# Turns of blocks: products with the identity matrix become TensorE transposes

## What is computed

```python
h = rmsnorm(x) * (1 + sc1) + sh1                      # modulation from c @ w_ada
qkv, z, b, a, cq, ckv, kpe, gate_a, gate_b = split(h @ w_in)
y_a = gdn_branch(qkv, z, b, a, ...)                   # short conv, delta rule, gated norm, @ w_o_gdn
y_b = mla_branch(cq, ckv, kpe, ...)                   # latent attention, causal or over pages, @ w_o_mla
x = x + g1 * ((sigmoid(gate_a) * y_a + sigmoid(gate_b) * y_b) @ w_out)
h = rmsnorm(x) * (1 + sc2) + sh2
# experts: top 4 of 32, for each chosen expert e of a token
gu = h @ w_gu[e] + b_gu[e]
gt = minimum(gu[:, :1024], 7); up = clip(gu[:, 1024:], -7, 7)
y = ((up + 1) * gt * sigmoid(1.702 * gt)) @ w_dn[e] + b_dn[e]
x = x + g2 * sum(gate * y)
```

## Time and profile before

| | |
|---|---|
| median of 3 runs | 1608.9 us (1607.83 to 1614.73) |
| span of the profiled execution | 1606.7 us |
| TensorE busy | 1543.6 us, 96% |
| VectorE busy | 481.4 us, 30% |
| ScalarE busy | 343.8 us, 21% |
| moved by the transfers | 541.33 MB, mean 337 GB/s |

### The profile page before, as it was taken

One profiled execution on the slowest core, in us unless ns is written; L12 is line 12 of the kernel. 1 busy time (PEld: TensorE's weight loads), 2 busy tenths in 40 slices (PEclk: granted clock), 3 DMA queues, 4 the chain that ended last, 5 costly groups with the idle time before them and its releaser, 6 DMA issues.

```text
span 1606.7 us, 25500 instructions
## 1 busy us (share of the span) xinstructions
PE 1543.6 (96%) x10185; PEld 845.6 (53%) x10185; DVE 481.4 (30%) x1079; ACT 343.8 (21%) x795; POOL 6.8 (0%) x13
## 2 busy tenths in 40 slices
PE   6999899999999999999999999999999999999997
PEld 4888786776677687434343343343343333333333
DVE  1665456322301025312221222122222212212224
ACT  2333452223311102111111111111111111111113
POOL 0000000000000000000000000000000000000000
PEclk9999999999999999999999999999999999999999
DMA  9748442545499964699999999999999999999991
GB/s 396 323 157 356 182 159 90 226 135 156 138 316 351 350 285 187 262 381 428 429 428 428 430 427 428 429 428 429 427 428 430 427 428 429 424 420 425 425 419 62
DMA packets 60259, 541.33 MB, mean 337 GB/s; under 512 B 7298, under 2 KB 11906, under 8 KB 29346
## 3 DMA queue, kind: packets, MB, share of 16 engines
q1 hardware_dynamic: 59474, 534.65, 81.0%
q0 software_dynamic: 720, 5.76, 0.9%
HBM read 533.54 MB, written 6.84 MB: 336 GB/s over the span
## 4 chain that ended last, share of the span: by engine, by line
PE 72%; DMA 21%; DVE 2%; SPq 2%; issue 2%; ACT 1%; ACTq 0%; DVEq 0%
DMA regC<-biases 20%; PE banks L606 14%; PE banks L558 10%; PE banks L1323 9%; PE banks L873 5%; PE banks L508 4%; PE banks L520 2%; PE banks L594 2%; PE banks L576 2%; PE banks L1156 2%; PE banks L1088 2%; PE banks L972 2%; PE banks L533 1%; DMA ring<-wpre 1%; PE banks L1181 1%
## 5 line engine op out<-in xcount | busy, mean ns | idle before, releaser
L558 PE MATMUL banks<-ring,regA 128*64 128x512 f32 x2024 | 446.8, 594 | 0.7 <-ACT regA L631 0.7
L558 PEld LDWEIGHTS banks<-ring,regA 128*64 128x64 f32 x2024 | 142.2, 137 | 281.9 <-issue 280.9
L606 PE MATMUL banks<-ring,regC 128*64 128x512 f32 x1024 | 226.8, 596 | 0.0
L668 DVE TENSOR_TENSOR regB<-regB,banks 128x528 f32<-128x528 f32 x128 | 81.5, 700 | 351.9 <-PE banks L533 351.9
L606 PEld LDWEIGHTS banks<-ring,regC 128*64 128x64 f32 x1024 | 70.7, 137 | 131.8 <-issue 127.9
L634 ACT ACTIVATE regA<-regA 128x512 f32<-128x512 f32 x32 | 20.1, 630 | 527.5 <-DVE regA L689 527.5
L689 DVE TENSOR_SCALAR regA<-banks 128x512 f32<-128x512 f32 x32 | 22.1, 692 | 347.0 <-PE banks L576 347.0
L508 PE MATMUL banks<-regC,regA 128*64 128x512 f32 (+1 forms) x396 | 97.1, 607 | 0.0
L873 PE MATMUL banks<-hT,ring 128*128 128x264 f32 x384 | 86.5, 387 | 0.0
L873 PEld LDWEIGHTS banks<-hT,ring 128*128 128x128 f32 x384 | 72.7, 190 | 12.7 <-issue 0.4
L533 PE MATMUL banks<-regA,regC 64*128 64x264 f32 x512 | 71.7, 409 | 0.0
(11 more groups left out here) (476 smaller groups left out, 1625.6 us busy)
## 6 DMA issues: line engine op xcount, KB each, us to landing
ring<-w_gu SPq DMA_DIRECT2D x126, 2048.0 KB, 17.6
ring<-w_dn SPq DMA_DIRECT2D x64, 2048.0 KB, 14.4
ring<-wpre SPq DMA_DIRECT2D x41, 2048.0 KB, 12.9
ring<-kvT SPq DMA_DIRECT2D x64, 256.0 KB, 4.8
ring<-kv SPq DMA_DIRECT2D x64, 256.0 KB, 6.2
ring<-ssm SPq DMA_DIRECT2D x2, 2048.0 KB, 15.4
o_ssms<-ring POOLq DMA_DIRECT2D x2, 2048.0 KB, 7.3
regC<-w_gu SPq DMA_DIRECT2D x1, 2048.0 KB, 9.2
```

The costliest lines, as they stand in the source:

```text
L558: mm = pe_mm(bank[x // 2][SLOT * (x % 2):SLOT * (x % 2 + 1), :], lhsT=hg[:, k % 4, SLOT * (k // 4):SLOT * (k // 4 + 1)], rhs=weights_k[:, ...
L606: mm = pe_mm(bank[5][SLOT * y:SLOT * (y + 1), :], lhsT=actT[:, m % 4, SLOT * (m // 4):SLOT * (m // 4 + 1)], rhs=ring[c][:, D * (m % 4) + H ...
L668: V.tensor_tensor(pair, pair, banks[:, b:b + 2, 0:T], ALU.add).then_inc(acc_added, 1)
```

## The change

Ten places that turn blocks of 128 x 128 by a product with `ident` call `pe.transpose` instead, with the same operands, banks, semaphores and order. Turns of narrower blocks, or onto part of the partitions (L587, L1073, L1276, L1352, L1421, L1447), stay products.

```diff
@@ turn_gathered (expert items)
-                    mm = pe_mm(bank[3][:, P * q:P * (q + 1)], lhsT=gtok[:, P * q:P * (q + 1)], rhs=ident, start=True, stop=True)
+                    mm = pe.transpose(bank[3][:, P * q:P * (q + 1)], gtok[:, P * q:P * (q + 1)], ident)
@@ item(j)
-                    pe_mm(bank[6][:, P * i:P * (i + 1)], lhsT=selg[:, i, :, :].rearrange("p a s -> p (a s)"),
-                          rhs=ident, start=True, stop=True)
+                    pe.transpose(bank[6][:, P * i:P * (i + 1)], selg[:, i, :, :].rearrange("p a s -> p (a s)"), ident)
...
-                        mm = pe_mm(bank[4 - 2 * y][:, P * q:P * (q + 1)], lhsT=act_[:, P * q:P * (q + 1)], rhs=ident, start=True, stop=True)
+                        mm = pe.transpose(bank[4 - 2 * y][:, P * q:P * (q + 1)], act_[:, P * q:P * (q + 1)], ident)
@@ turn_mod
-                pe_mm(bank[b][:, at:at + P], lhsT=mrow[:, i % 2, :], rhs=ident, start=True, stop=True).then_inc(mod_turned, 1)
+                pe.transpose(bank[b][:, at:at + P], mrow[:, i % 2, :], ident).then_inc(mod_turned, 1)
@@ turn_tokens_of (delta rule)
-                        mm = pe_mm(bank[2 + g][:, i * P:(i + 1) * P], lhsT=qkvT[:, H * (1 + w) + 4 * g + i, tok], rhs=ident,
-                                   start=True, stop=True)
+                        mm = pe.transpose(bank[2 + g][:, i * P:(i + 1) * P], qkvT[:, H * (1 + w) + 4 * g + i, tok], ident)
@@ L1118, L1238, L1351, L1370, L1387
-                mm = pe_mm(bank[2][:, P * g:P * (g + 1)], lhsT=ksr[:, g, :], rhs=ident, start=True, stop=True)
+                mm = pe.transpose(bank[2][:, P * g:P * (g + 1)], ksr[:, g, :], ident)
...
-                        mm = pe_mm(bank[4 + g][:, P * k:P * (k + 1)], lhsT=qrow[:, g, P * k:P * (k + 1)], rhs=ident, start=True, stop=True)
+                        mm = pe.transpose(bank[4 + g][:, P * k:P * (k + 1)], qrow[:, g, P * k:P * (k + 1)], ident)
...
-                    pe_mm(bank[2 + g // 4][:, P * (g % 4):P * (g % 4 + 1)], lhsT=ps_[q][:, P * g:P * (g + 1)], rhs=ident, start=True, stop=True)
+                    pe.transpose(bank[2 + g // 4][:, P * (g % 4):P * (g % 4 + 1)], ps_[q][:, P * g:P * (g + 1)], ident)
...
-                    mm = pe_mm(bank[7][:, P * k:P * (k + 1)], lhsT=orow[:, P * k:P * (k + 1)], rhs=ident, start=True, stop=True)
+                    mm = pe.transpose(bank[7][:, P * k:P * (k + 1)], orow[:, P * k:P * (k + 1)], ident)
...
-                mm = pe_mm(bank[7][:, P * g:P * (g + 1)], lhsT=osr[:, P * g:P * (g + 1)], rhs=ident, start=True, stop=True)
+                mm = pe.transpose(bank[7][:, P * g:P * (g + 1)], osr[:, P * g:P * (g + 1)], ident)
```

## The result

The changed kernel takes 1600.35 us (median of 13 runs, 1597.19 to 1605.53). The kernel before takes 1613.17 us in the runs beside it, where the front of this document had 1608.9 from three. The ratio is 0.9921, with an interval of 0.9908 to 0.9935: 12.7 us less, between 10.5 and 14.8. One of the 13 runs of the kernel before took 5547.14 us; it is left out of the ratio and hardly moves the median. The forecast was 1598.8 us or 0.9937.

The account below looks back on a forecast made before the run. TensorE's own work bounds the kernel up to about 640 us, full weight transfers the later expert items. Savings of 4.7 + 3.5 + 1.95 = 10.1 us bring the 1608.9 median to 1598.8 us, range 1593.5 to 1602.5.

Parts of the forecast that it names:

- The price of a turn: Everywhere: a transpose takes one record where a product takes two, saving 0.11 us per turn on the path.
- The turns outside the delta layer: Before 130 us and after 230 us: 42 turns on the path at 0.111 us, 4.7 us saved.
- The items: 32 expert items: TensorE saves 0.55 us each, but full transfers hide most; 1.95 us counts in all.
- the restart: Transfers restarting at 702.79 us, behind items 0 and 1: reached 1.1 us sooner.
- the closed gap: Transfer gap just before 702.79 us, costing 1.9 us: nearly closes, 0.3 us counted.
- The delta layer: 130 to 230 us: 41 turns, 4.8 us on paper; 3.5 taken between bounds 2.1 and 8.4, because of two stalls.
- Rival (b): Stall at 172.91 us shrinks or goes, or gap at 703 closes: 1592.5 to 1596 us; chance 0.09.
- The signs named: Trace checks, such as first L558 at about 638 instead of 646.4; forecast wrong if granted clock drops in items.
- Rival (d): Expert items: longer bias waits lower the clock, costing 1.7 us in every item; about 1620 us, chance 0.05.
- (a): Delta-layer stalls keep all they can and the restart wins only 1.1 us: 1601 us; chance 0.20.
- (c): Expert items stay bound by TensorE, so the 29 others give 0.55 us each too: 1583 us; chance 0.01.
- (e): Changed turns: the transpose form still makes two passes, 1608 to 1609 us; chance 0.03.

Follow-up runs that it names:

- e_pad: Changed kernel with nine unread 64x64 products put in ahead of the delta layer's first block; 1602.67 us.
- e_items: Kernel before with the transposes in the expert items alone, including the four of the first gather; 1611.47 us, ratio 0.9990.
- e_late: Kernel before with the first 2 MB z-projection chunk held back until the delta layer's first block is nearly through; 1607.12 us, one run.
- e_narrow: Kernel before, no transposes, with the items' scatter products 80 columns narrower, so TensorE waits longer; 1613.24 us, one run.
- e_double: Changed kernel with each of the items' turns made twice over as transposes; 1599.59 us.
- e_fill: Changed kernel with five unread products of 264 columns ahead of the wait for the bias in each item; 1643.07 us.
- e_again: Changed kernel run again, unaltered, for a second trace; 1599.94 us, ratio 0.9920.
- e_bias: Changed kernel with each item's bias load issued ahead of its last two weight chunks instead of behind them; 1593.60 us, ratio 0.9887.

## Why the prediction was right

**The price of a turn** held: 0.109 us a transpose in L1349, one record. The Trainium skill, "TensorE: Matmul & The Clock Gate", section Terms, has the transpose mode four times faster for FP32. The trace does not agree: L1349 took 0.87 us for what took 1.78 as products with the identity, which is twice as fast.

**The turns outside the delta layer** were forecast at 4.7 us. The stages show 4.2 in attention (36 turns, forecast 4.0) and 0.5 in the router (19.9 to 19.4 where the clock stays up; forecast 0.44 for the four of L520). The two of L812 at the start are lost in a scatter of 124.8 to 129.4 us.

**The items** were forecast at 1.95 us for all 32, although 0.55 each is won on TensorE. Measured: 1.8 (936.1 to 934.3, and 934.2 in e_pad). Of its terms the restart gave 1.1 as forecast (55.3 us behind the first L558 instead of 56.4), and with the last item's 0.55 only 0.2 is left for the closed gap, where I had 0.3. L593 comes 0.85 us ahead of L605 in the item shown, where 1.0 was named. The period is 29.69 us with 1.37 us of wait, as named, and the first wait shows in item 7 (at 856.64 us, counted from 0), as named too.

**The delta layer** is the mis-sized term: 3.5 us taken, 4.2 between the medians of the traces, 7.3 between the two that happened to be compared. The sum on paper was 4.8, and I cut it because I took the end of the transfers for what ends the stall. That step was wrong (e_items, e_late): the stalls end 2.3 to 2.5 us behind a packet of the instruction queue, with the transfers full or dry. The other half of my sentence, that the same place in the instruction stream is reached further on in the work and the stall may shrink, was right (record 1734). That 3.5 us came near all the same is luck: it was a value between bounds of 2.1 and 8.4, chosen for the wrong reason. Rival (b)'s condition came true in the trace, where the stall shrank from 3.60 to 1.11 us, but not its time: 3.60 is the longest of the five stalls seen at this place in the old code (2.33 to 3.60), and the edited stage had 1.00 to 2.48.

With these the sum is 4.2 + 0.5 + 1.8 + 4.2 = 10.7 us where the forecast had 10.1, and the timed difference is 12.7 (10.5 to 14.8). The forecast's ratio of 0.9937 lies just outside the measured interval (0.9908 to 0.9935). The forecast time came within 1.6 us because two deviations cancel: the kernel before was 4.3 us slower beside it, and the gain 2.6 us larger.

Part of the larger gain may be the clock. In the 44 runs of the kernel before beside the experiments, the time goes with the run's mean granted clock: 1606.93 to 1610.06 us in the seven at 0.995, 1612.17 to 1614.11 in the six at 0.991, 1614.40 to 1618.87 in the seven below 0.989. The profiled execution of before is one at 0.995, that of the changed kernel one like its median (0.983). A difference of the two traces, 8.1 us, so leaves out what before's median run lost to falls.

**The signs named** came out but for two. The first L558 moved by 6.3 us and not by 8.4, because this trace has the fall of the clock in the router (3.6 us) and a start 2.0 us late, and a delta layer 3.8 us shorter than the forecast had it. And "wrong if the granted clock drops in items": it dropped, and the time was still right.

**Rival (d)** is therefore half true. The longer wait for the bias does bring falls of the clock (e_narrow, e_double, e_fill), in one item and not in the next, as in the timeline above. What it loses in such an item (1.64 us in L508 alone) comes near the price I had given it, 1.7 us. But I had let every item pay. An item that pays takes up the next one's wait, which is 0.10 us there instead of 1.37, and the period stays 29.69 us. The stage is 934.2 to 934.3 us in the changed kernel, e_again and e_pad, to a tenth what the sum without falls gives, so the falls cost nothing that shows. The same page of the Trainium skill, Part 4: PE-mode transpose, says that transposes do not engage the full clock. Here e_double ran twice as many of them at 1.00 in every window from 700 to 1500 us, and e_narrow had the falls without them; the traces speak against it.

**Rivals (a), (c) and (e)** fell: the stall didn't keep its share; the items' period didn't move; each transpose is one record.

## What to carry to other kernels

Ask of each saved microsecond whether the transfer stream is already continuous behind it; if so, only what lies ahead of its last gap and behind its last landing counts. What lands last is then worth more than what TensorE does: one small load moved ahead of two large ones won 5 us, three times what 32 x 10 faster turns did. And a stall that the program does not explain may belong to a place in the instruction stream: count instructions up to it in two kernels before calling it chance. Compare stages over several traces before a difference of 3 us is put down to an edit.

## What the hardware showed unasked

- A product of 264 float32 columns is two records, 0.22 us each; five of them lengthened an item by 2.4 us, not 1.1 (e_fill).
- In and behind runs of tiny products (64x64, 0.035 us each) TensorE stands still for 1.0 to 3.6 us at fixed counts of its records (1608 or 1609, 1734 or 1735, some 126 apart), and goes on 2.3 to 2.5 us after a 16 KB packet of the instruction queue starts, with the transfers full or not.
- The router's stage ran at a clock of 1.00 or 0.84 with the same code there (e_pad, e_again), which is worth 3.6 us; with work put into the wait ahead of it, it was still 0.84 in one trace.
- A fall of the clock behind a wait can pay for itself: it takes up the next wait, and the next item keeps the clock. Waits of 0.98 to 1.37 us ahead of the bias products brought falls; of 0.80 there, or of 1.2 ahead of L560's full products (e_bias), they didn't.
